# Attention of a one-step transformer kernel: the next head's query projection cut into halves and its key projection moved, over the units of a head

## What is computed

```python
q = (rmsnorm(q_a, q_norm) @ w_qb).reshape(B, S, N_HEADS, QK_DIM)      # 256 -> 8 heads of 96
q_nope, q_rope = q[..., :QK_NOPE_DIM], q[..., QK_NOPE_DIM:]
kv = (keys_ckv @ w_kvb).reshape(B, K, N_HEADS, QK_NOPE_DIM + V_HEAD_DIM)
s = (q_nope . k_nope + q_rope . k_rope) * ATTN_SCALE
p = softmax(s)                                                        # in float32
attn = p @ v
```

## Time and profile before

| | us |
|---|---|
| median of 3 runs | 1420.73 |
| lowest, highest | 1420.66, 1421.64 |
| span of the profiled execution | 1419.9 |

### The profile page before, as it was taken

The page is one execution under the profiler, slowest core; times in us unless marked ns, Lnnn a source line. Parts: engine busy times, 40 slices in busy tenths (PEclk is TensorE's granted clock), DMA queues, the critical chain, the costliest instruction groups (busy, mean ns, idle before and its releaser), DMA issues.

```text
span 1419.9 us, 20517 instructions
## 1 busy us (share of the span) xinstructions
PE 1371.5 (97%) x7548; PEld 1232.9 (87%) x7548; DVE 806.2 (57%) x1201; ACT 701.2 (49%) x1409; POOL 434.2 (31%) x533
## 2 busy tenths in 40 slices
PE   7999989999999899999999999999999999999996
PEld 2899878999888878899998889999999999999995
DVE  4777677787768655245554456544435565344444
ACT  4867578787777633243333443433334443333332
POOL 3366648888878444440000001200000030000002
PEclk9999999999999999999999999999999999999998
DMA  9431101111111150164344333433333334333321
GB/s 347 144 99 53 35 25 43 42 43 28 35 38 38 55 221 1 60 236 148 148 162 149 119 119 119 165 141 122 118 126 126 127 126 162 125 139 119 118 89 45
DMA packets 50493, 154.63 MB, mean 109 GB/s; under 512 B 9848, under 2 KB 12440, under 8 KB 50424
## 3 DMA queue, kind: packets, MB, share of 16 engines
q1 hardware_dynamic: 49560, 150.60, 29.9%
q0 software_dynamic: 864, 3.15, 0.5%
HBM read 148.73 MB, written 4.83 MB: 108 GB/s over the span
## 4 chain that ended last, share of the span: by engine, by line
PE 63%; POOL 1%; DMA 0%; DVE 0%; issue 0%; ACT 0%; SPq 0%; DVEq 0%; POOLq 0%
PE bank L2071 28%; PE bank L2079 28%; PE bank L1792 7%; PE bank L1554 1%; DMA x<-in_w_o 0%; POOL x L1862 0%; PE bank L2093 0%; POOL stat L1866 0%; POOL stat L1886 0%; DVE wol L1749 0%; ACT woh L1718 0%; SPq L1674 0%; DVE x L2022 0%; DVE xn L2010 0%; POOL stat L1868 0%
## 5 line engine op out<-in xcount | busy, mean ns | idle before, releaser
L2071 PE MATMUL bank<-h2h,w1l 128*128 128x384 f32 x768 | 258.3, 336 | 0.0
L2071 PE MATMUL bank<-h2l,w1h 128*128 128x384 f32 x768 | 258.2, 336 | 0.0
L2071 PE MATMUL bank<-h2h,w1h 128*128 128x384 f32 x768 | 258.2, 336 | 0.0
L1862 POOL TENSOR_TENSOR x<-x,xn 128x512 f32<-128x512 f32 x12 | 20.6, 1747 | 726.5 <-DVE rTl L1980 499.8
L1969 DVE TENSOR_TENSOR w2l<-w2raw,w2h 128x1024 fp32r<-128x1024 f32 x95 | 118.6, 1249 | 169.5 <-ACT w2h L1900 169.5
L1900 ACT ACTIVATE w2h<-w2raw 128x1024 fp32r<-128x1024 f32 x95 | 100.8, 1061 | 191.3 <-PE bank L2079 191.3
L1907 ACT ACTIVATE relu<-bank 128x384 f32<-128x384 f32 x94 | 46.2, 491 | 287.6 <-PE bank L2071 287.6
L2079 PE MATMUL bank<-w2h,rTh 128*128 128x512 f32 x576 | 181.8, 396 | 0.0
L2079 PE MATMUL bank<-w2l,rTh 128*128 128x512 f32 x576 | 179.3, 392 | 0.0
L2079 PE MATMUL bank<-w2h,rTl 128*128 128x512 f32 x576 | 178.2, 390 | 0.0
L1976 DVE TENSOR_TENSOR sq<-relu 128x384 f32<-128x384 f32 x96 | 57.1, 595 | 179.6 <-ACT relu L1907 174.7
(11 more groups left out here) (273 smaller groups left out, 2777.1 us busy)
## 6 DMA issues: line engine op xcount, KB each, us to landing
w1raw<-in_w SPq DMA_DIRECT2D x96, 512.0 KB, 3.8
w2raw<-in_w SPq DMA_DIRECT2D x96, 512.0 KB, 4.6
ada_raw<-in_w_ada SPq DMA_DIRECT2D x24, 512.0 KB, 5.6
xn<-in_w_ada SPq DMA_DIRECT2D x16, 512.0 KB, 3.7
xin<-in_x SPq DMA_DIRECT2D x9, 512.0 KB, 4.5
x<-in_x SPq DMA_DIRECT2D x3, 1536.0 KB, 9.3
g_raw<-in_w_ada SPq DMA_DIRECT2D x8, 512.0 KB, 3.9
x<-in_w_o SPq DMA_DIRECT2D x6, 512.0 KB, 5.8
```

What stands on the lines that cost most here:

```text
L1862: nc.gpsimd.tensor_tensor(k.x[:, t, cut], k.x[:, t, cut], gated_half(t, i), ALU.add).then_inc(out_added, 1)
L2071: op = nc.tensor.matmul(bank[6 + s][:, 0:BN], w[0][s][x][:, c * P:(c + 1) * P], k.h2[b % 2][y_][:, c, :], start=n == 0, stop=n == 3 * DC - 1)
```

## The change

The key columns are cut in another order: item 1 now has the 256 last columns, item 2 columns 512 to 1024. Query items 0 and 1 are made in two halves, each of three products (one step of K = 256), in consecutive units: the first half at x = 1 and 5 (`half_of`), the second at x = 2 and 6, where `SIDE_AT` has the item. Key item 2 moves from x = 5 to x = 4; query item 1 from x = 4 to x = 5 and 6, item 0 from x = 1 to x = 1 and 2. Query item 2 stays whole at x = 7. In `ring` an item in halves has the place of its first half. All that ACT and POOL do with items 0 and 1 follows `SIDE_AT`, so it comes later: item 0 is read by ACT at x = 3 (was 2) and item 1 at x = 7 (was 5), and so on. POOL's `turn_query` has one more wait, for `q_lo`.

Products per unit of a head:

| x | before | after |
|---|---|---|
| 0 | key 512 | key 512 |
| 1 | query, 6 products | query, 3 |
| 2 | none | query, 3 |
| 3 | key 512 | key 256 |
| 4 | query, 6 | key 512 |
| 5 | key 256 | query, 3 |
| 6 | none | query, 3 |
| 7 | query, 6 | query, 6 |

```diff
-        KCUT = ((0, 512), (512, 1024), (1024, NKEY))
-        SIDE_AT = {0: ("k", 0), 1: ("q", 0), 3: ("k", 1), 4: ("q", 1), 5: ("k", 2), 7: ("q", 2)}
+        KCUT = ((0, 512), (1024, NKEY), (512, 1024))
+        SIDE_AT = {0: ("k", 0), 2: ("q", 0), 3: ("k", 1), 4: ("k", 2), 6: ("q", 1), 7: ("q", 2)}
+        HALF_AT = {1: 0, 5: 1}
...
+        def half_of(u):
+
+            h, x = divmod(u, LT)
+            return ("q", 3 * (h + 1) + HALF_AT[x]) if x in HALF_AT and h + 1 < H else None
+
+        def in_halves(item):
+
+            return item[0] == "q" and item[1] % 3 in HALF_AT.values()
...
-            if side_of(u):
+            if half_of(u):
+                ring.append(half_of(u))
+            if side_of(u) and not in_halves(side_of(u)):
                 ring.append(side_of(u))
...
                 def turn_query(n, u):
                     f = qf[n % 2]
                     pool.wait_ge(rs_ready, 2 * u)
+                    pool.wait_ge(q_lo, n)
                     pool.wait_ge(q_nope, n + 1)
...
+                def query_half(n, b, d):
                     h, c = divmod(n, 3)
                     cut = slice(c * BN, (c + 1) * BN)
+                    for i, (x, y) in enumerate(((0, 0), (0, 1), (1, 0))):
+                        op = nc.tensor.matmul(b[:, 0:BN], wh[h % 2][x][:, d * P:(d + 1) * P], k.qnT[y][:, d, cut],
+                                              start=d == 0 and i == 0, stop=d == 1 and i == 2)
+                    return op
+
+                def project_query(n, b, filled):
+                    query_half(n, b, 0)
+                    query_half(n, b, 1).then_inc(filled, 1)
...
-                    if side:
+                    if side and in_halves(side):
+                        query_half(side[1], ring_bank(*side), 1).then_inc(side_filled, 1)
+                    elif side:
                         ring_free(pe, *side)
...
+                    half = half_of(u)
+                    if half:
+                        ring_free(pe, *half)
+                        query_half(half[1], ring_bank(*half), 0)
```

More of the change, by code:

```diff
@@ L1356, in columns @@
                     op.then_inc(cols_done, 1)
-                def project_query(n, b, filled):
+                def query_half(n, b, d):
                     h, c = divmod(n, 3)
                     cut = slice(c * BN, (c + 1) * BN)
[L1361 to L1367, removed]
+                    for i, (x, y) in enumerate(((0, 0), (0, 1), (1, 0))):
[5 more added lines that the diff above has]
+                    query_half(n, b, 1).then_inc(filled, 1)
                 def project_key(n, b, filled):
```

## The result

| | median, us | runs |
|---|---|---|
| before | 1421.51 (1418.94 to 1425.59) | 20 |
| changed | 1423.85 (1421.44 to 1425.82) | 20 |

The ratio is 1.0017, with a 95% interval of 1.0011 to 1.0024: slower by 2.3 us in the medians (1.6 to 3.4 by the interval), where 1.5 us less was forecast. That is within what the prediction calls "same", and above its range, which ended at 1422.2.

The account below looks back on a forecast made before the run. TensorE, busy 97%, was taken as the bound, with each unit held to a floor by its exponent chain. Gains of 5.85 less costs of 4.45 gave 1.4 to 1.5 us off, 1419.2 us; range 1415.9 to 1422.2.

Parts of the forecast that it names:

- same: Whole kernel: a measured time within about 0.2% (2.8 us) of no change; chance 0.62.
- x=4: Units at x=4: DVE reads the smaller key item 1 out sooner; gain 0.45 to 0.7 a head, 4.1 us.
- the floor: Each unit's chain from its scores through DVE's maximum and ACT's exponent to the next scores: 4.3 to 4.6 us.
- x=2 and x=6: Added query halves fit TensorE's gaps there at no cost, except 0.52 us in unit 18.
- x=1: Units lose half a query item: 1.45 us gained, less 0.1 in three heads for gated x=2 starts: 1.15.
- x=3: Units with the smaller key item, held by their own exponent: at most 0.08 a head, 0.2 us gained.
- rival C: POOL's subtraction and turning at x=0 make ACT late at x=1 in all seven heads: 1425.2 us, chance 0.07.
- the model of x=4: Unit 28, head 3: query product stood 0.64 us until DVE had read key item 1's bank; gain 0.7.
- ACT and the bank: ACT gains 0.4 us in unit 6; later rounding costs 0.65, banks held over two units 0.5 and 0.4.
- POOL's queue: Item 2's turning comes behind a subtraction: 1.0 us lost in unit 9, 1.35 in unit 17, together 2.4.
- A: POOL's queue doesn't bite, units 9 and 17 keep their length, bank reads in time: 1416.3 us, chance 0.25.
- B: Gaps overfilled by 0.1 in fourteen units and gain at x=4 stops at 0.35: 1421 us, chance 0.13.

Follow-up runs that it names:

- e8_bank: Changed kernel with POOL turning query item 2 before subtracting item 1, and the first half's ring place and products behind the context product: 1420.51 us, ratio 0.9992.
- e11_before_pool: Kernel before plus one unused 128x384 POOL subtraction ahead of query item 2's turning at x=0, in seven heads: 1422.21 us, ratio 1.0005.
- e3_kcut: Kernel before with only the key columns cut in the new order, queries as before: 1421.49 us, ratio 0.9999.
- e10_bank_ada: e8_bank with modulation block 1 started in unit 8 instead of 7: 1419.70 us, ratio 0.9991.
- e1_swap: Changed kernel with POOL at x=0 turning query item 2 before it subtracts item 1: 1420.14 us, ratio 0.999.
- e19_fill: Changed kernel with nine more TensorE products, results overwritten, ahead of the first half in units 9 and 17: 1420.83 us, ratio 0.9995.
- e4_whole: Changed kernel without halves, query items 0 and 1 whole at x=2 and x=6: 1424.59 us, ratio 1.0025.
- e17_best: Changed kernel without halves, query item 0 whole at x=1, item 1 at x=6, item 2 turned first, modulation block 1 in unit 8: 1421.59 us, ratio 1.0001.
- e5_q1early: Changed kernel with query item 1's halves at x=4 and 5 and key item 2 at x=6: 1432.26 us, ratio 1.0074.

## Why the prediction was wrong

The forecast was 1.45 us less; units 4 to 55 of the two traces say 2.1 more, 3.5 us apart. Two terms make up nearly all of it: x=4 gave 1.8 less than summed, and 1.5 lie in unit 10 at the lowered clock, for which the sum had nothing. Point by point, in these units:

- **What bounds the kernel, and the floor.** Right. x=2 and x=6 took the added products with changes of 0.03 to 0.13 and of 0.0 to -0.06; x=1 gained 1.1 in heads 3 to 6 (1.45 before the deduction) and x=3 gained 0.7, half a microsecond more than the 0.2 given; the gated starts of x=2 (those that wait for the exponent) cost 0.4 where 0.3 was given.
- **x=4: mis-sized, the first step that failed.** 2.3 us for 4.1. The prediction worked x=4 out from the size of the key items alone and put the SBUF port that DVE and POOL share at nothing. Five heads gave 0.5 to 0.7, as worked out. Units 20 and 44 became longer by 0.4 and 0.5 instead of shorter. DVE's scaling of the output, which stands ahead of their maximum, took 2.03 us ahead of unit 20's maximum where it had taken 1.07 (DVE and POOL, changed kernel):

```profile
273.11 2.03 DVE L1278 TENSOR_TENSOR attn<-ropeq,out_l 64x512 f32<-64x512 f32 x1
...
272.99 1.29 POOL L642 TENSOR_TENSOR xn<-krT 128x512 f32<-128x512 f32 x1 [0.17 <-POOL krT L630]
```

  and in the kernel before:

```profile
271.48 1.07 DVE L1265 TENSOR_TENSOR attn<-ropeq,out_l 64x512 f32<-64x512 f32 x1
...
271.56 2.08 POOL L629 TENSOR_TENSOR xn<-krT 128x512 f32<-128x512 f32 x1 [0.17 <-POOL krT L617]
```

  Whichever started first ran at its usual length (1.07 or 1.29), the other 0.8 to 1.0 longer. Three scalings took over 1.6 us in the kernel before and four in the changed one, each with a POOL instruction under way at its start. No edit was made to test it, but traces that differ in it agree: in the second one of the changed kernel unit 20's scaling took 1.69, 0.34 less, and unit 20 was 0.35 shorter; in e8_bank unit 44's took 1.21 for 1.92, and unit 44 is 4.63 for 5.35. The prediction had quoted the rule for it (the Trainium skill, SBUF — State Buffer, "SBUF: two separate sides") beside rival C and left it out of the sum. These rows agree with the rule, within 0.2 us: by an estimate from the starts and lengths shown, the second would have ended after 2.24 and 2.28 us if it waited out the first, where 2.03 and 2.08 were measured. What should have been in the sum is that a shift of 0.1 us decides who pays.
- **Unit 28, the model of x=4, was such a case itself.** Its 0.7 came out, but not for the reason given. In the kernel before, the scaling in it ran behind a POOL instruction:

```profile
308.50 1.78 DVE L1265 TENSOR_TENSOR attn<-ropeq,out_l 64x512 f32<-64x512 f32 x1
...
308.39 1.02 POOL L597 TENSOR_TENSOR ql<-qf,qh 128x384 fp32r<-128x384 f32 x1
```

  and in e11_before_pool, which leaves keys and queries where they were, ahead of it:

```profile
310.27 1.08 DVE L1268 TENSOR_TENSOR attn<-ropeq,out_l 64x512 f32<-64x512 f32 x1
...
310.30 1.89 POOL L597 TENSOR_TENSOR ql<-qf,qh 128x384 fp32r<-128x384 f32 x1
```

  There the 0.64 us before the query product are gone and unit 28 is 4.95, as short as in the changed kernel (4.92), whose scaling took 1.07 as well. The key cut alone (e3_kcut, scaling still 1.77) gives 0.19. Where the changed order meets the collision again (e10_bank_ada, 1.83 us) unit 28 is 5.12. So the 0.64 us that the prediction read as a wait for the bank were for the most part POOL's, and the full 0.7 is partly luck.
- **ACT and the bank: right, within 0.4.** x=7 +0.1 in five heads, units 39 and 47 +0.42 each, unit 40 took it back (-0.46); unit 6 -0.4; unit 18 +0.6 for 0.52; units 24 and 32 +0.12 each, less than half of what was given. Not foreseen: x=5 +0.02 to +0.13, 0.5 in all.
- **POOL's queue: right in place, short in price.** Units 9 and 17 +0.92 and +1.69, for 1.0 and 1.35; ACT's wait in unit 9 1.50, in unit 17 1.61. e1_swap takes it away again, and e11_before_pool makes that of unit 9 alone. No other head pays.
- **The second step that failed: what such a wait does next.** The sum charged ACT's lateness as time on the path, and nothing for TensorE standing idle meanwhile. The idle time grew to 1.9 and 2.05 us, and the clock fell behind one of the two in the first trace, behind both in the second. e19_fill shows it: filled, the clock stays, and the whole kernel is about 3 us faster. Without the lowered clock the changed kernel would still be 0.6 us over the kernel before in these units, not 1.45 under: x=4 is 1.8 short, x=5 0.5 and unit 17 0.3 over, and x=3 gives 0.5 back.
- **The rivals.** A (the queue doesn't bite) is out. B (the change gives nothing it says) is wrong in cause, since the gaps held; only its smaller gain at x=4 came in part, for another reason. Its number was added wrongly too: its costs of 1.4 + 1.8 on top of the forecast of 1419.2 make 1422.4, not 1421, and that lies above the stated range. C, at 1425.2, came nearest in time as the numbers stood, and by luck: its price, 1.2 a head, was real in the two heads of the forecast and in none of the five others.
- **The range** was worked out from terms at full clock; its upper end, 1422.2, had no room for 1.5 to 3 us of clock.

## What to carry to other kernels

A gap of TensorE that an exponent chain ends is not room for gain: read the floor (what the next start waits for) first, and price evening out at the distance to it. When a step moves, list every in-order queue it moves in, also those of engines that are idle a fifth of the stage (POOL, busy 200.9 of 255.4 us): there the last customer before a deadline pays, and long background blocks (here 5.8 us, with up to 3 us of wait for their load ahead of them) belong behind the short steps that others wait for. Before a unit's length is explained by the wait that ends last in it, compare the durations in it with those of other units: an instruction at 1.78 us for 1.07 is the first thing to explain. Give a new stall of TensorE of about 2 us a second outcome, with a stretch at half clock, and a chance for it; fill it if it can't be removed.

## What was not expected of the hardware

- Behind the idle times of TensorE of 1.93 to 2.05 us in the two traces of the changed kernel the granted clock was 0.50 (1.2 GHz) in three of four cases, and score products were 0.32 us apart instead of 0.175; each case cost about 1.5 us. Over all traces, nine idle times of 1.9 to 2.5 us stand between units 4 and 55 and five are followed by it (the others that are: 2.24 us in e4_whole and 2.25 in e17_best; that are not: 2.37 in e4_whole and twice 2.45 in e5_q1early). In e11_before_pool a lowered stretch stood behind an idle time of 1.23 us (in unit 43), while 1.28 us before unit 10 had none. So the length of the idle time alone doesn't decide it, and what does stays open here.
- DVE's scaling (64x512) and POOL's addition (128x512) ran one after the other: 1.07 and 2.08 us, or 2.03 and 1.29, by which started first. One such collision made unit 28 of the kernel before 0.7 us longer than it had to be.
